# Differential attention of the second block: scores and output products in pairs of f16 halves, with the transposed probabilities copied once before they are split

## What is computed

```python
def diff_attention(q, k, v, rel_bias, lam, lam_init, subln_w):
    ...
        logits = jnp.einsum('bqhmd,bkhmd->bhmqk', q_blk, k).astype(jnp.float32) * scale + bias
        p = jax.nn.softmax(logits, axis=-1)
        attn = p[:, :, 0] - lam * p[:, :, 1]
        return jnp.einsum('bhqk,bkhd->bqhd', attn.astype(v.dtype), v)
    ...
    o = rmsnorm(o, subln_w) * (1.0 - lam_init)
```

## Time and profile before

| | |
|---|---|
| time, median of 3 runs | 2670.35 us (2670.31 to 2670.37) |
| profiled execution, first to last instruction | span 2668.5 us |
| PE matmul busy | 2656.6 us, 100% of the span |
| DVE busy | 1822.5 us, 68% |
| ACT busy | 1337.7 us, 50% |
| chain that ended last | PE 97%, DVE 1% |

### The profile page before, as it was taken

The page is one execution under the profiler, slowest core; times in us unless marked ns, Lnnn a source line. Parts: engine busy times, 40 slices in busy tenths (PEclk is TensorE's granted clock), DMA queues, the critical chain, the costliest instruction groups (busy, mean ns, idle before and its releaser), DMA issues.

```text
span 2668.5 us, 45121 instructions
## 1 busy us (share of the span) xinstructions
PE 2656.6 (100%) x17772; PEld 1741.6 (65%) x17772; DVE 1822.5 (68%) x2792; ACT 1337.7 (50%) x2284; POOL 136.5 (5%) x119
## 2 busy tenths in 40 slices
PE   9999999999999999999999999999999999999999
PEld 6886476654688646886476654688646556465664
DVE  7995385666899528994385665899526786557854
ACT  5664265552566425663265542566424654336452
POOL 1000012100100001000022100100000002000020
PEclk9999999999999999999999999999999999999999
DMA  5443321223344333443322223444323232321312
GB/s 170 115 121 107 122 80 59 88 67 104 91 120 116 116 98 95 121 115 107 122 80 67 81 74 104 116 125 111 121 100 119 72 95 72 111 84 64 111 64 87
DMA packets 313358, 266.23 MB, mean 100 GB/s; under 512 B 8796, under 2 KB 276316, under 8 KB 312576
## 3 DMA queue, kind: packets, MB, share of 16 engines
q1 hardware_dynamic: 310192, 254.31, 30.8%
q10 hardware_dynamic: 2416, 7.84, 1.1%
q0 software_dynamic: 608, 2.11, 0.3%
HBM read 257.40 MB, written 4.21 MB: 98 GB/s over the span
## 4 chain that ended last, share of the span: by engine, by line
PE 97%; DVE 1%; DMA 0%; DVEq 0%; ACT 0%; SPq 0%; issue 0%; ACTq 0%
PE pu L473 15%; PE pu L475 15%; PE pu L474 15%; PE pm L473 6%; PE pm L475 6%; PE pm L474 6%; PE pu L596 6%; PE pu L598 6%; PE pu L597 6%; PE pm L596 2%; PE pm L598 2%; PE pm L597 2%; PE pm L912 2%; PE pm L668 2%; PE pm L898 1%; PE pm L926 1%
## 5 line engine op out<-in xcount | busy, mean ns | idle before, releaser
L1105 DVE SCALAR_TENSOR_TENSOR w_lo<-stage,w_hi 128x2048 f16<-128x2048 f32 (+1 forms) x152 | 342.9, 2256 | 367.0 <-ACT w_hi L1885 363.3
L1885 ACT ACTIVATE w_hi<-stage 128x2048 f16<-128x2048 f32 (+1 forms) x143 | 265.9, 1859 | 529.4 <-PE pm L475 377.9
L473 PE MATMUL pu<-h_hi,w_hi 128*128 128x512 f16 x912 | 346.3, 380 | 0.0
L475 PE MATMUL pu<-h_hi,w_lo 128*128 128x512 f16 x912 | 345.6, 379 | 0.0
L474 PE MATMUL pu<-h_lo,w_hi 128*128 128x512 f16 x912 | 345.6, 379 | 0.0
L473 PE MATMUL pu<-w_hi,arena 128*128 128x512 f16 x512 | 194.0, 379 | 0.0
L474 PE MATMUL pu<-w_lo,arena 128*128 128x512 f16 x512 | 194.0, 379 | 0.0
L475 PE MATMUL pu<-w_hi,arena 128*128 128x512 f16 x512 | 194.0, 379 | 0.0
L473 PE MATMUL pm<-w_hi,arena 128*128 128x512 f16 x512 | 194.0, 379 | 0.0
L474 PE MATMUL pm<-w_lo,arena 128*128 128x512 f16 x512 | 194.0, 379 | 0.0
L475 PE MATMUL pm<-w_hi,arena 128*128 128x512 f16 x512 | 194.0, 379 | 0.0
(11 more groups left out here) (345 smaller groups left out, 6222.4 us busy)
## 6 DMA issues: line engine op xcount, KB each, us to landing
stage<-in_w_in_dram SPq DMA_DIRECT2D x144, 512.0 KB, 4.5
stage<-in_w_ffn_gate_dram SPq DMA_DIRECT2D x88, 512.0 KB, 3.9
stage<-in_w_ffn_up_dram SPq DMA_DIRECT2D x88, 512.0 KB, 5.1
stage<-in_w_ffn_down_dram SPq DMA_DIRECT2D x80, 512.0 KB, 4.0
stage<-in_w_out_dram SPq DMA_DIRECT2D x40, 512.0 KB, 4.2
stage<-in_w_ffn_down_dram SPq DMA_DIRECT2D x16, 256.0 KB, 4.2
stage<-in_w_branch_hgrn_dram SPq DMA_DIRECT2D x8, 512.0 KB, 3.4
stage<-in_w_branch_attn_dram SPq DMA_DIRECT2D x8, 512.0 KB, 4.6
```

The lines of the kernel that those rows point to most:

```text
L473: nc.tensor.matmul(ps, w1, r_hi, start=first, stop=False)
L475: return nc.tensor.matmul(ps, w2, r_hi, start=False, stop=last)
L1105: V.scalar_tensor_tensor(out=w_lo[:, s, 0:n], in0=stage[:, s, 0:n], scalar=WSCALE, in1=w_hi[:, s, 0:n], op0=ALU.mult, op1=ALU.subtract).th ...
L1885: A.activation(w_hi[:, s, 0:n], stage[:, s, 0:n], ACT.Copy, scale=WSCALE).then_inc(hi_split, 1)
```

## The change

Queries, keys and values of the differential heads are written as f16 halves when their units are evacuated: ACT writes the high half (`halves2`, new semaphore `part_hi`), DVE the low half, where DVE alone wrote float32 before. `scores2` makes three f16 matmuls for each `m` instead of one in float32, and `head_out2` 48 f16 matmuls instead of 16 in float32. `taken` first copies the transposed probabilities from PSUM to `wide` (float32, which signals `pt_ready`), then writes their high half from `wide` (`pt_hi`); DVE writes the low half (`probs_low`, `pt_lo`). The scale `SS` undoes the factors, in `softmax2` and in the copy of the output. The retention heads keep the float32 product, now called `head_out_wide`.

```diff
+SPLIT2 = ("aq", "ak", "av")
+SS = 1.0 / (ASCALE * ASCALE)
...
+        wide = gp[:].rearrange("p (a b) -> p a b", a=2)
...
             def scores2(i):
...
-                    r = slice(64 * m, 64 * m + 64)
-                    last = nc.tensor.matmul(pm[2 * (i % 2) + m][:], daq[r, hd, b * P:(b + 1) * P], dak[r, hd], start=True, stop=True)
+                    last = part(m, 0)
+                for j in (1, 2):
+                    for m in order:
+                        last = part(m, j)
                 last.then_inc(sc_done, 1)
...
+            def head_out2(ps, v_hi, v_lo, hd):
+
+                pairs = (AT_hi, v_hi), (AT_hi, v_lo), (AT_lo, v_hi)
+                for b in range(NB):
+                    for kb in range(NB):
+                        for j, (l, r) in enumerate(pairs):
+                            last = nc.tensor.matmul(ps[:, b * P:(b + 1) * P], l[:, kb, b * P:(b + 1) * P], r[:, kb, hd * P:(hd + 1) * P],
+                                                    start=kb + j == 0, stop=kb == NB - 1 and j == 2)
                 last.then_inc(o_done, 1)
...
-                    pe.wait_ge(pt_ready, t.next("pt_ready", 4))
-                    pe.wait_ge(p_ready, t.now("p_ready"))
+                    t.next("pt_ready", 4)
+                    pe.wait_ge(pt_lo, t.next("pt_lo", 4))
                     if q < 17:
-                        pe.wait_ge(p_ready, t.now("p_ready") + 1)
+                        pe.wait_ge(mx_ready, t.at("mx_ready", q))
...
-                    V.tensor_tensor(Lm[:, m], pm[2 * (i % 2) + m][:], toep[:, hd, first:first + T], ALU.add)
+                    V.scalar_tensor_tensor(out=Lm[:, m], in0=pm[2 * (i % 2) + m][:], scalar=SS, in1=toep[:, hd, first:first + T], op0=ALU.mult, op1=ALU.add)
...
+            def probs_low(i):
+
+                v.wait_ge(pt_hi, t.next("pt_hi"))
+                c = slice(i % NB * P, (i % NB + 1) * P)
+                V.scalar_tensor_tensor(out=AT_lo[:, :, c], in0=wide[:, i % 2].rearrange("p (k c) -> p k c", k=NB), scalar=ASCALE, in1=AT_hi[:, :, c],
+                                       op0=ALU.mult, op1=ALU.subtract).then_inc(pt_lo, 1)
...
                 between()
+                if q in (4, 8, 12, 16):
+                    probs_low(q - 1)
                 if q < 16:
                     probs2(q)
+                    if q not in (0, 4, 8, 12):
+                        probs_low(q - 1)
...
-                if kind in ("av", "bv"):
+                if kind in SPLIT2:
+                    v.wait_ge(part_hi, t.next("part_hi"))
+                    for out_hi, out_lo, bank, scale in halves2(kind, part, banks):
+                        last = V.scalar_tensor_tensor(out=out_lo, in0=bank, scalar=scale, in1=out_hi, op0=ALU.mult, op1=ALU.subtract)
+                    last.then_inc(evac, 1)
+                elif kind in ("av", "bv"):
...
-                A.activation(AT[:, :, b * P:(b + 1) * P], pm[2 * (i % 2)][:].rearrange("p (k c) -> p k c", k=NB), ACT.Copy).then_inc(pt_ready, 1)
+                if i >= 2:
+                    s_.wait_ge(pt_lo, t.at("pt_lo", i - 1))
+                A.activation(wide[:, i % 2], pm[2 * (i % 2)][:], ACT.Copy).then_inc(pt_ready, 1)
+                s_.drain()
+                A.activation(AT_hi[:, :, b * P:(b + 1) * P], wide[:, i % 2].rearrange("p (k c) -> p k c", k=NB), ACT.Copy, scale=ASCALE).then_inc(pt_hi, 1)
...
                 for n, (kind, part) in enumerate(MIX2_ORDER):
+                    if kind in SPLIT2:
+                        banks = ((set_a, pu)[l] if n < 2 else pu)[2 * (n % 2):2 * (n % 2) + 2]
+                        s_.wait_ge(unit_done, t.now("unit_done") + 1)
+                        for out_hi, _, bank, scale in halves2(kind, part, banks):
+                            last = A.activation(out_hi, bank, ACT.Copy, scale=scale)
+                        last.then_inc(part_hi, 1)
```

More of the change, by code:

```diff
@@ L115 @@
             pt_ready=16, o_rc=8, o_done=8, o_sq=8, o_rt=8, o_rb=8, o_cp=8, m_ready=12, rot_ready=2, rot_land=64, dup_land=32, ret_done=16, ret_ready=16, pw_land=16,
+            part_hi=6, pt_hi=16, pt_lo=16,
             pool_sum=1, pool_in=4, pool_done=4, pool_free=1, x_ready=4, rx=4, xn_ready=4, tp_done=8, hh_ready=8, h_ready=8)
@@ L256, in build_program @@
         AT = f32(93.25, NB, T)
+        (daq_hi, daq_lo), (dak_hi, dak_lo) = ((v[:, 0::2], v[:, 1::2]) for v in (f16(0, 8, T), f16(8, 8, T)))
+        AT_hi, AT_lo = f16(93.25, NB, T), f16(97.25, NB, T)
+        dV_hi, dV_lo = f16(16, NB, T), f16(20, NB, T)
+        wide = gp[:].rearrange("p (a b) -> p a b", a=2)
         rel_hot, rel_row = f32(0, 2 * T)[0:32], f32(85, 2 * T)[0:A_HEADS]
@@ L345, in build_program @@
         rot_ready = sem("rot_ready")
+        part_hi = sem("part_hi")
+        pt_hi = sem("pt_hi")
+        pt_lo = sem("pt_lo")
         rot_land = sem("rot_land")
@@ L362, in build_program, with halves2 @@
         end_half = sem("end_half")
+        def halves2(kind, part, banks):
+            dst = {"aq": (daq_hi, daq_lo), "ak": (dak_hi, dak_lo), "av": (dV_hi, dV_lo)}
+            out_hi, out_lo = dst[kind]
+            scale = DS * ASCALE * (0.125 if kind == "aq" else 1.0)
+            if kind in ("av", "bv"):
+                cols = slice(part * 256, part * 256 + 256)
+                return [(out_hi[:, b:b + 2, cols], out_lo[:, b:b + 2, cols], banks[b // 2][:].rearrange("p (b c) -> p b c", b=2), scale) for b in (0, 2)]
+            return [(out_hi[:, 2 * part + e], out_lo[:, 2 * part + e], banks[e][:], scale) for e in range(2)]
         x_in = a["x"].rearrange("(b p) d -> p b d", p=P)
@@ L889, in scores2, with part @@
                 hd, b = divmod(i, NB)
-                for m in (1, 0) if i in (8, 12) else (0, 1):
+                parts = (daq_hi, dak_hi), (daq_hi, dak_lo), (daq_lo, dak_hi)
+                def part(m, j):
+                    r = slice(64 * m, 64 * m + 64)
+                    return nc.tensor.matmul(pm[2 * (i % 2) + m][:], parts[j][0][r, hd, b * P:(b + 1) * P], parts[j][1][r, hd], start=j == 0, stop=j == 2)
+                order = (1, 0) if i in (8, 12) else (0, 1)
+                for m in order:
                     if m == 0 and i >= 2:
@@ L907, in transpose2, with head_out_wide @@
                 last.then_inc(pt_done, 1)
-            def head_out2(ps, v_tok, hd):
+            def head_out_wide(ps, v_tok, hd):
                 for b in range(NB):
@@ L913, in head_out2 @@
                                                 start=kb == 0, stop=kb == NB - 1)
+                last.then_inc(o_done, 1)
+            def head_out2(ps, v_hi, v_lo, hd):
[5 more added lines that the diff above has]
+                                                    start=kb + j == 0, stop=kb == NB - 1 and j == 2)
                 last.then_inc(o_done, 1)
@@ L930, in mixer2_slot @@
                 if q in (5, 9, 13, 17):
-                    pe.wait_ge(pt_ready, t.next("pt_ready", 4))
-                    pe.wait_ge(p_ready, t.now("p_ready"))
+                    t.next("pt_ready", 4)
+                    pe.wait_ge(pt_lo, t.next("pt_lo", 4))
                     if q < 17:
-                        pe.wait_ge(p_ready, t.now("p_ready") + 1)
+                        pe.wait_ge(mx_ready, t.at("mx_ready", q))
                     else:
                         pe.wait_ge(o_cp, t.next("o_cp"))
-                    head_out2(pm[1], dV, (q - 5) // 4)
+                    head_out2(pm[1], dV_hi, dV_lo, (q - 5) // 4)
                 if 1 <= q <= 16:
@@ L963, in mixer2_slot @@
                         head_turn(pm[1], tc[:, (hd - 1) % 2])
-                    head_out2(pm[0], bV, hd)
+                    head_out_wide(pm[0], bV, hd)
                 if q == POOL_SLOT:
@@ L2239, in mixer2_slot @@
                     s_.wait_ge(o_done, t.next("o_done"))
-                    A.activation(tc[:, k % 2], ps[:], ACT.Copy).then_inc(o_sq, 1)
+                    A.activation(tc[:, k % 2], ps[:], ACT.Copy, scale=SS if k < A_HEADS else 1.0).then_inc(o_sq, 1)
                 if 1 <= q <= 16 and q not in (8, 12):
```

## The result

The changed kernel takes 2686.37 us, median of 4 runs (2685.0 to 2688.47), against 2670.34 of before (2670.31 to 2670.37): ratio 1.0061, 95% interval 1.0048 to 1.0073. It is 0.6% slower, where the prediction said 2680.5 in a range of 2673 to 2692. The profiled execution took 2685.0 with a span of 2683.2, 14.7 us more than before. The runs of before lie within 0.06 us of each other and those of after within 3.5. This scatter is a second finding; the profiled run is the fastest of the four and shows no cause for it.

What follows compares the result with a forecast made beforehand. TensorE, busy 2656.6 of 2668.5 us, was taken as the bound. 13.8 us less work against some 24 us of new waits adds 10.4, giving 2678.9, with 1.85 beyond the span 2680.7; stated 2680.5, range 2673 to 2692.

Steps and rivals of the forecast that it cites:

- the saving: On PE, scores and output products together: 13.8 us less work.
- what PE loses: New waits on PE in the attention stretches of two layers: some 24 us.
- Output products: Each head's output product on PE falls from 3.57 to 2.68 us, 7.1 us saved in eight heads.
- Rival E: Narrow output products go at a weight load's pace, 99 ns: 9.4 us lost instead of 7.1 saved, 2697; chance 0.03.
- Scores: Score step on PE falls from 1.15 to 0.94 us, 6.7 us saved in 32 slots.
- Rival C: f16 score pairs on the two row halves don't run together: about 2691 us; chance 0.10.
- The order on ACT: In slots 0, 2 and 6 DVE waits for high halves behind ACT's exponentials; slot 2's lap grows from 6.07 to 10.3 us.
- The laps: DVE's time per slot: 8.4 us in slot 0, 7.2 in a unit's first slot, 10.3 in slot 2, 8.0 in slot 4.
- Behind slot 8: After scores 8, 8.1 us late, 4.2 come back and 1.3 are lost again: a layer ends 5.2 us late.
- the fifth point: Sign in the attention stretch: the time is lost by slot 8, and some comes back in heads 2 to 4.
- rival D: Clock falls in PE's longest waits, before scores 4 and 8; four places cost 4 to 8 us: 2687; chance 0.08.
- the five places named: PE idles before scores of slots 2, 4, 8 (1 us or more) and transposes of slots 2, 6 (about 1 us).

Runs made afterwards that it cites:

- the three traces above: Changed kernel unfilled, with idle-time matmuls ahead of slots 4 and 8, and ahead of slots 2, 4 and 8: 2686.37, 2685.27 and 2685.03 us.
- the run for slots 0 and 2: Changed kernel with ACT writing the unit's high halves ahead of the exponentials in slots 0 and 2 alone: 2675.64 us.
- the run with slot 8 filled: Changed kernel with 12 f16 matmuls, overwritten later, ahead of the scores of slot 8 alone: 2685.02 us.
- output products alone: Changed kernel with only the output products in f16 pairs; queries, keys and scores stay float32: 2678.38 us.

## Why the prediction was right, and what was mis-sized

The mechanism was the one forecast: waits behind the order on ACT. The price was 4.3 us low in the profiled run (2680.7 against 2685.0), and 5.7 against the median. Part of the agreement is luck: the saving was sized 3.3 us too small, and what PE loses 7.6 us too small (24.2 us, where 17.1 + 14.7 = 31.8 were lost). Of these, 26.0 us stand in the trace as waits in the two layers; the rest lies in the slow step behind slot 4 (1.4 to 1.5 us a layer) and in the 0.1 to 0.3 us that other steps with a wait last beyond 6.47 us and their waits.

**Output products.** 2.67 us, 0.0556 us for each matmul, as the earlier trace rows gave. The Trainium skill, "TensorE: Matmul & The Clock Gate", section "Back-to-back issue gap", has about 81 ns for such a stream; this trace disagrees with it. Rival E is out.

**Scores.** The step was sized too small: 1.15 to 0.94 us was predicted, and by the slot without a wait (6.78 to 6.47) it saves 0.31, 9.9 us in all instead of 6.7. With 7.2 for the output products PE has 17 us less to do. The six products span 0.82 us, so pairs on the two row halves run together; six in turn would span 1.46 (five distances of 0.216 and a last one of 0.38). Rival C is out. Up to slot 8 DVE's laps set the time, so the saving of the scores does not reach it there; that is my reading of the chain, and agrees with the 68 us from scores 0 to scores 8 in the three traces above.

**The order on ACT.** DVE idles for L2324 in slots 0, 2 and 6, and starts the low halves 6.88 us after the scores in slot 2 (6.9 predicted). Putting those instructions first gives back 18.8 us. This is shown by experiment. By the medians, some 1.4 of the 18.8 are the slow clock behind slot 8, which goes with the long wait there: against the 2685.02 with that wait filled it is 17.5.

**The laps: the step that was mis-sized.** From DVE's start on slot 0 to that on slot 7 the prediction has 59.8 - 1.0 = 58.8 us, the trace 60.67, 1.9 more. Scores 8 are accordingly 9.9 us late instead of 8.1. The parts: slot 1 to 2 has 7.32 instead of 7.2. `probs_low` costs 0.84 us there: its own 0.68, and 0.16 until the next instruction starts. When DVE arrives late it no longer hides this gap under a wait for the scores; I had 0.65. Slots 0, 2, 3, 4 and 5 are 0.13 to 0.30 over for the same and smaller reasons, 1.1 in sum. Slot 6 has 10.95 instead of 10.3, because ACT is late for its exponentials:

```profile
2111.02 1.28 ACT L1962 ACT_TABLE_LOAD   x1
2112.31 0.30 ACT L1962 ACTIVATE r_col<-r_col,eps 128x4 f32<-128x4 f32 x1
2112.63 1.28 ACT L2294 ACT_TABLE_LOAD   x1
2113.92 0.72 ACT L2294 ACTIVATE ta<-ta,small 128x512 f32<-128x512 f32 x1
```

The head's squares, a square root and two table loads stand ahead of them. The exponentials start 3.27 us behind DVE's start here (2113.92 against 2110.65), 2.87 in slot 2: 0.40 of the 0.65. Before, ACT had 1.66 us to spare at this place; my lap took the exponentials as 4.4 us behind the start in every slot and did not look at what else ACT has in slot 6. No run takes that work away, so its share is read from the trace, not shown.

**Behind slot 8.** PE regained 2.95 us by the next layer, where 4.2 - 1.3 = 2.9 was predicted. That this fits so well is luck: at 0.31 us a slot the saving is 4.9, and the waits ahead of slots 11 and 12 take 1.8 (0.76 and 1.05). Head 2 gave nothing back, though the fifth point had some come back in heads 2 to 4. The second layer added 7.7 us, the first 7.0. The predicted 5.2 plus the 1.9 of the laps makes 7.1. The second layer's 0.7 more are mostly a wait of 0.34 us ahead of slot 15 and a step from slot 9 to slot 10 that is 0.23 longer.

**The clock, rival D.** It had 0.08 and happened in part. In the profiled run the falls cost nothing. In others the fall makes the step behind slot 8 longer by 1.6 to 3.0 us (8.42 - 6.78 and 9.44 - 6.48). Later waits take back part of it: by the scores of slot 12 it costs 1.2 to 2.4 us a layer (32.28 and 33.55 us from scores 8 to scores 12 in the run for slots 0 and 2, 31.12 in the changed kernel's profile). The median of the four runs is 1.4 us above what the kernel takes with that wait filled (2685.02). So of the 16.0 us over before about 14.7 are waits less PE's saving, and 1.4 the clock. Rival D put the price on four places, slots 4 and 8 of each layer; only slot 8 carries it. That each run above 2686 had its fall at slot 8 is argued from the scatter that goes away: only the profiled run has a trace.

**Checks.** A slot without a wait 6.47 us (6.57 predicted); PE's waits 12.8 us in the first layer (11 to 13 predicted): 10.2 at the five places named, 2.6 ahead of the scores of slots 3, 11 and 12. DVE starts on slot 3 at 2087.34, 6.1 us later than before (2081.27). The clock did fall below 1 behind one of the waits named. The prediction had called that a sign of being wrong, and on this point it was wrong, though in the profiled run it cost nothing.

## What to carry to other kernels

When work is moved to an engine with a free third, add up its lap in each slot against the period of the engine that bounds, and look at the queue: an instruction that another engine waits for, put behind something that arrives late, costs its whole wait, however short it is. Here three pairs of copies in the wrong place cost 18.8 us in two layers (1.4 of it by the clock), more than the 17 us of which PE had been relieved, and moving them made a slower kernel a slightly faster one. A wait's length is its cost only if what follows is not itself waiting; the same slow clock was free ahead of a lap that was late anyway and cost 1.2 to 2.4 us where PE set the pace.

## What was not expected of the hardware

- An idle time of PE of 1.9 to 3.4 us, in a stretch where it is otherwise busy, was followed in some traces by a granted clock of 0.50 for 3 to 6 us, and in others not: in the run with slot 8 filled, the waits of 1.93 and 2.65 us ahead of slots 2 and 4 left it at 1.00. The changed kernel gave 2685.0 and 2688.5. Twelve idle-time matmuls ahead of slot 8 made it 2685.02, within 0.2 us.
- The scatter of some us between runs was the sign of the slow clock, in a kernel whose own profiled run showed no fall that cost. The wait ahead of slot 8 was itself the same, 3.40 to 3.42 us, in a trace without a fall behind it (the changed kernel) and in two with one (output products alone; high halves first in slots 0 and 2).
- GpSimd subtracted 128x512 into f16 in 1.16 to 1.69 us, 1.24 in the mean. Two L1699 on DVE, which read PSUM, took 1.29 us beside it, as without it; a `scalar_tensor_tensor` that reads `r_post` and `arena` took 1.65 us instead of 0.75.
